# A hybrid decoder layer with mixture of experts on one core: sample states stored in eight pieces, step rows sent home one step later, the samples' chunk of the end added on VectorE

## The chip, the cores and the metric

The kernel runs on 1 core of a Trainium2 chip. The metric is the device time of one execution in microseconds, lower is better. TensorE does the matmuls (PE in the rows, PEld its weight loads), VectorE is DVE, ScalarE is ACT, GpSimd is POOL, SyncE is SP. SPq and POOLq are the queues of these engines where they issue DMAs.

## The reference, cut to what matters

One layer, 1024 prompt tokens and 8 sample tokens of 1024 features, all in float32. A mixer (mLSTM heads and HGRN2 heads) comes first and updates, for the 8 samples, two matrix states of 4 heads, C and S, which are outputs. Then comes the mixture of experts, whose sum with the scaled input is normalised:

```python
x = _layer_norm(DEEPNORM_ALPHA * x + mix, ln1_g, ln1_b)
x = _layer_norm(DEEPNORM_ALPHA * x + _hmoe(x, ...), ln2_g, ln2_b)
...
a = jnp.einsum('nd,edf->nef', xt, w1)
u = jnp.einsum('nd,edf->nef', xt, w3)
hdn = jax.nn.silu(a) * u * gate[..., None].astype(x.dtype)
return jnp.einsum('nef,efd->nd', hdn, w2).reshape(B, T, D)
...
S_new = jnp.exp(G_end[:, :, 0, :])[..., None] * S + jnp.einsum('bhsc,bhsv->bhcv', k * jnp.exp(G_end - G), i)
```

Each token takes 2 of 16 experts (the other gates are zero), and an expert has three weights (gate, up, down) of 1 MB each.

## The kernel before

The first two thirds of the time are the mixer, the first layer norm and the router; the change does not touch them. What follows has two parts.

**The steps.** Pairs of token and expert are sorted by expert into tiles of 32 rows. 80 tiles make 20 steps (0 to 19) of four lanes: a step takes 128 rows, 32 on each of four streams, and each stream has its own expert. TensorE's order in step n (`tensor_moe`, `step`) is: gate product of n (L1359), transposes of the hidden rows of n-1 (L1345), transposes of the gathered rows of n+1 (L1321), down product of n-1 (L1336), up product of n (L1370). Weights have one buffer for each stream, so a load may be issued only when the product of the step before has read its buffer.

SyncE's order in step n (`sync_moe`, `step`) is: read the experts and flags of n+1 from SBUF into registers (`experts_of`, L1232), wait for gate product n, issue the four gate loads of n+1 (L1220), in even steps below 16 also the samples' v rows (`load_v`, L1241); read the experts of n, wait for down product n-1, issue the four down loads of n (L1226); wait for up product n, issue the four up loads of n+1 (L1223). Each of these loads has a flag: it moves its 1 MB only if the stream changes its expert there, so many issues move nothing. All of SyncE's DMAs are on one queue.

GpSimd (`pool_moe`) issues indirect DMAs: it gathers the rows of step n (L1460), then sends home the finished rows of step n-4 (`send_home`, L1453: 128 rows of 4 KB into the DRAM tensor `y_rows`). A send waits for VectorE's sum of its step (L1584) and for the send before it. There are four buffers for finished rows. ScalarE fills the one of step n (`scale_x`, L1407) once step n-4 has arrived home, and the gather of n+2 waits for that fill. ScalarE's next instruction is the SiLU of step n (L1417).

VectorE updates four heads' worth of the sample states at the end of each of the steps 0 to 15 (`update_state`, L1593 to L1595): C in steps 0 to 7, S in steps 8 to 15. Each is 2 MB, 16 KB on each partition. C is stored whole ahead of step 8 and S ahead of step 16 (`between`, L1277 to L1284, issued in the helper at L470), each after a wait for the last of its updates. Ahead of step 12 the parameters of the last layer norm are loaded (L1281).

**The end.** When all 20 sends have arrived, SyncE loads nine chunks of pairs of rows (L1295): the 8 sample rows first, then eight chunks of 128 tokens, 1 MB each. TensorE adds the two rows of a pair by products with the identity (L1383), 4 products of 512 columns a chunk, each with two records in the trace, and VectorE takes the statistics (L1633, L1635) and centres (L1636); ScalarE and GpSimd finish chunks 0 to 6 in that order, VectorE the last two (L1639), and SyncE stores them.

Of the kernel before, what the change touches and what calls it, by code (L numbers as in the profile page):

```python
# [20 lines left out]
ALU = mybir.AluOpType  # L21
# [10 lines left out]
H = 4  # L32
DV1 = P + 1
PIECE = NT // 3
HB = H * NS
LEVELS = [64, 32, 16, 8, 4, 2, 1]
NLEV = len(LEVELS)
NTT = NCH + 1
# [10 lines left out]
STEPS = (2 * NT + NE * (ROWS - 1)) // ROWS // STREAMS  # L49
# [61 lines left out]
def _program(nc, t, ctx):  # L111
# [15 lines left out]
    PS = ctx.enter_context(nc.psum_tensor("psum", [P, 8, 512], F32))  # L127
# [5 lines left out]
    ident, ones = const("ident"), const("ones")  # L133
# [335 lines left out]
    def out_dma(eng, dst, src):  # L469
        eng.dma_start(dst, src).then_inc(s.outputs, 16)  # L470
        outs[0] += 1
# [41 lines left out]
    def x_rows(c):  # L513
        return P if c < NCH else NS
# [699 lines left out]
    def sync_moe(sp):  # L1214
        wg = t["w_gate"].rearrange("e (p k) f -> e p k f", k=KD)
        wu = t["w_up"].rearrange("e (p k) f -> e p k f", k=KD)
        wd = t["w_down"].rearrange("e (p k) n -> e p k n", k=2)

        def load_gate(q, expert, new):
            sp.dma_start(w_gate[q], wg[bass.ds(expert, 1)].rearrange("e p k f -> p (e k) f"), cond=new).then_inc(s.w_gate_in, 16)  # L1220

        def load_up(q, expert, new):
            sp.dma_start(w_up[q], wu[bass.ds(expert, 1)].rearrange("e p k f -> p (e k) f"), cond=new).then_inc(s.w_up_in, 16)  # L1223

        def load_down(q, expert, new):
            sp.dma_start(w_down[q], wd[bass.ds(expert, 1)].rearrange("e p k n -> p (e k) n"), cond=new).then_inc(s.w_down_in, 16)  # L1226

        def experts_of(n):

            def words(w, top):  # L1230
                row = step_loads[0:1, bass.ds((n * 2 + w) * STREAMS, STREAMS)]
                return nc.values_load_multi_w_load_instructions(row, engines=[mybir.EngineType.SP], min_val=0, max_val=top,  # L1232
                                                                skip_runtime_bounds_check_because="experts are minima with NE - 1, flags come from a comparison")[1]

            experts, flags = words(0, NE - 1), words(1, 1)
            return [(q, experts[q], flags[q]) for q in range(STREAMS)]

        def load_v(piece):
            if piece >= 1:
                sp.wait_ge(s.state_added, 2 * piece)  # L1240
            sp.dma_start(v_piece, v_dram[piece:piece + 1].rearrange("a (b v) -> a b v", b=NS).partition_broadcast(P).rearrange("p a b v -> p (a b) v")).then_inc(s.v_piece_in, 16)  # L1241

        sp.wait_ge(s.experts_known, 1)
        sp.wait_ge(s.mixed, NTT)
        first = experts_of(0)
        for q, expert, _ in first:
            load_gate(q, expert, None)
        sp.wait_ge(s.slots_part, AFTER_SPREAD[0] + 1)
        for q, expert, _ in first:
            load_up(q, expert, None)  # L1250
        for q, expert, _ in first:
            load_down(q, expert, None)
        early_outs.append(outs[0])

        def step(pair, i, last):
            n = pair * 2 + i
            if not (last and i == 1):
                coming = experts_of(n + 1)
                sp.wait_ge(s.gate_done, pair * 2 + (i + 1))
                for q, expert, new in coming:  # L1260
                    load_gate(q, expert, new)
                if i == 0 and pair < 2 * H:
                    load_v(pair)
            if not is_first(pair, i):
                present = experts_of(n)
                sp.wait_ge(s.down_done, n)
                for q, expert, new in present:
                    load_down(q, expert, new)
            if not (last and i == 1):
                sp.wait_ge(s.up_done, pair * 2 + (i + 1))  # L1270
                for q, expert, new in coming:
                    load_up(q, expert, new)

        def between(pair):

            if pair == 4:
                sp.wait_ge(s.outputs, 16 * early_outs[0])  # L1277
                sp.wait_ge(s.state_added, 8)
                out_dma(sp, t["out_C_s"].rearrange("p h b v -> p (h b) v"), C0)
            elif pair == 6:  # L1280
                sp.dma_start(ln2_gb, t["ln2"].partition_broadcast(P)).then_inc(s.ln2_in, 16)  # L1281
            elif pair == 8:
                sp.wait_ge(s.state_added, 16)
                out_dma(sp, t["out_S_s"].rearrange("p h b v -> p (h b) v"), S0)  # L1284

        for pair in range(STEPS // 2):
            between(pair)
            for i in range(2):
                step(pair, i, pair == STEPS // 2 - 1)
        sp.wait_ge(s.outputs, 16 * outs[0])  # L1290
        sp.wait_ge(s.y_out, 16 * STEPS)
        homes = y_rows[0:SPARE].rearrange("(k n) d -> n k d", k=2)
        for n, c in enumerate(ROW_ORDER):
            r = x_rows(c)
            sp.dma_start(pair_of[c][0:r], homes[c * P:c * P + r]).then_inc(pair_in[n], 16)  # L1295
        for n, c in enumerate(ROW_ORDER):
            r = x_rows(c)
            if n < Y_SHIFTED:
                sp.wait_ge(s.y_ready, n + 1)
            else:  # L1300
                sp.wait_ge(s.y_last, NCH + n - Y_SHIFTED)
            out_dma(sp, t["out_y"][c * P:c * P + r], pair_of[c][0:r, 0])
        sp.wait_ge(s.outputs, 16 * outs[0])

    def tensor_moe(pe):
# [67 lines left out]
        pairs_loop(pe, step)  # L1373
        turn_hid(STEPS - 1)
        down(STEPS // 2 - 1, 1)
        for n, c in enumerate(ROW_ORDER):
            r = x_rows(c)
            pe.wait_ge(pair_in[n], pair_there[n])
            if n >= 4:
                pe.wait_ge(s.y_centred, n - 3)  # L1380
            for half in range(2):
                for k in range(2):
                    m = mm(PS[0:r, 2 * (n % 4) + half, :], ident[0:r, 0:r], pair_of[c][0:r, k, half * 512:(half + 1) * 512], start=(k == 0), stop=(k == 1))  # L1383
            m.then_inc(s.y_summed, 1)

    def scalar_moe(act, link, tell):
# [52 lines left out]
    def pool_moe(pool, link, tell):  # L1439
        g = nc.gpsimd  # L1440
        pool.wait_ge(s.tiles_known, 1)
        pool.wait_ge(s.x1_written, 16 * NTT)

        pool.wait_ge(s.routed, NTT)
        pool.wait_ge(s.outputs, 16 * early_outs[0])

        def send_home(n):

            pool.wait_ge(s.y_read, 2 * n + 2)
            if n >= 1:  # L1450
                pool.wait_ge(s.y_out, 16 * n)
            off = bass.IndirectOffsetOnAxis(slot_home[:, n:n + 1].bitcast(U32), 0)
            g.indirect_dma_start(y_rows, off, ysb[n % YBUFS], None).then_inc(s.y_out, 16)  # L1453

        for n in range(STEPS):
            if n >= 2:
                pool.wait_ge(s.xg_turned, n - 1)
                pool.wait_ge(s.x_scaled, n - 1)
            off = bass.IndirectOffsetOnAxis(slot_tok[:, n:n + 1].bitcast(U32), 0)
            g.indirect_dma_start(xg[n % 2], None, x1_dram, off).then_inc((s.xg_in0, s.xg_in1)[n % 2], 16)  # L1460
            if n >= 4:
                send_home(n - 4)
        for n in range(STEPS - 4, STEPS):
            send_home(n)

        pool.wait_ge(s.ln2_in, AFTER_FIRST + 16)
        for n, c in enumerate(ROW_ORDER[:Y_SHIFTED]):
            y = pair_of[c][0:x_rows(c), 0]
            pool.wait_ge(s.lstd_ready, NTT + n + 1)
            tell(g.tensor_tensor(y, y, ln2_gb[0:x_rows(c), 1], ALU.add), s.y_ready)  # L1470

    def vector_moe(dve, link, tell):
# [154 lines left out]
        for n, c in enumerate(ROW_ORDER):  # L1627
            r = x_rows(c)
            y = pair_of[c][0:r, 0]
            summed = PS[0:r, 2 * (n % 4):2 * (n % 4) + 2, :].rearrange("p a b -> p (a b)")  # L1630
            dve.wait_ge(s.y_summed, NTT + n + 1)
            for half in range(2):
                i = v.bn_stats(fst[0:r, c, half], summed[:, half * 512:(half + 1) * 512])  # L1633
            link(i)
            tell(v.bn_aggr(fmv[0:r, c], fst[0:r, c]), s.moments)  # L1635
            tell(v.scalar_tensor_tensor(y, summed, fmv[0:r, c, 0:1], ln2_gb[0:r, 0], ALU.subtract, ALU.mult), s.y_centred)  # L1636
            if n >= Y_SHIFTED:
                dve.wait_ge(s.lstd_ready, NTT + n + 1)
                tell(v.scalar_tensor_tensor(y, y, fsd[0:r, c:c + 1], ln2_gb[0:r, 1], ALU.mult, ALU.add), s.y_last)  # L1639
# [474 lines left out]
```

## Time and profile before

| | us |
| --- | --- |
| median of 3 runs | 1168.73 (1166.11 to 1173.96) |
| the profiled execution, its own time | 1177.88 |
| its span | 1176.0 |
| granted TensorE clock, mean share | 0.935 |
| TensorE busy (share of the span) | 1051.2 (89%) |
| VectorE busy | 541.5 (46%) |
| ScalarE busy | 274.3 (23%) |
| GpSimd busy | 214.2 (18%) |

The span is from the first to the last instruction of the profiled execution; positions in the rows are microseconds from its start. The steps take from about 818 to 1124, the end the rest. In the chain of waits every row is a start, a length and what the end of the execution hung on at that time.

### The profile page before, as it was taken

The numbers are of one execution on the slowest core, as the hardware profiler recorded it, in microseconds if no ns is written. First come the engines' busy times: TensorE is split into PE (matmuls) and PEld (weight loads), VectorE is DVE, ScalarE is ACT, GpSimd is POOL, SyncE is SP. The second block draws the span as 40 slices with busy tenths as digits, with TensorE's granted clock in tenths as the row PEclk, the third lists the DMA queues.
The fourth block names the chain that finished last, engine by engine and source line by source line (L and its number), as shares of the span: only waits on it lengthen the run. The fifth ranks groups of instructions, "written<-read, shape, count | busy, mean of one in ns | idle before, by whom it ended". The sixth has DMA issues, their size and how long they took to land.

```text
span 1176.0 us, 17325 instructions
## 1 busy us (share of the span) xinstructions
PE 1051.2 (89%) x6814; PEld 618.9 (53%) x6814; DVE 541.5 (46%) x983; ACT 274.3 (23%) x557; POOL 214.2 (18%) x204
## 2 busy tenths in 40 slices
PE   7999999979999987999999999942788889898877
PEld 4666666646565545566666656542344445444423
DVE  1540033344645466776685667353133324332227
ACT  1542112122222223233333333110111111111103
POOL 0000000001111132443453354000111101110014
PEclk9999999989999988999999999965898889898968
DMA  9110102020000154001100010508898776846765
GB/s 383 44 72 1 72 1 72 0 76 1 1 1 1 34 214 181 3 18 37 37 18 19 37 36 19 191 33 347 333 353 299 262 285 196 339 161 223 260 250 201
DMA packets 29443, 150.11 MB, mean 128 GB/s; under 512 B 5338, under 2 KB 5786, under 8 KB 20034
## 3 DMA queue, kind: packets, MB, share of 16 engines
q1 hardware_dynamic: 23186, 123.94, 28.1%
q0 software_dynamic: 5760, 20.97, 4.9%
q10 hardware_dynamic: 432, 4.35, 1.0%
q8 instruction: 38, 0.62, 0.2%
q14 instruction: 27, 0.22, 0.1%
HBM read 317.32 MB, written 23.82 MB: 290 GB/s over the span
## 4 chain that ended last, share of the span: by engine, by line
PE 83%; DMA 7%; DVE 5%; issue 3%; SPq 2%; ACT 0%; POOL 0%; DVEq 0%; ACTq 0%; POOLq 0%
PE psum L1689 18%; PE psum L1740 9%; PE psum L772 9%; PE psum L785 8%; PE psum L1336 5%; PE psum L1359 5%; PE psum L1370 4%; PE psum L813 4%; PE psum L1383 3%; DMA weight_slots<-in_w_gate 2%; DMA hg_decay<-in_w_up 2%; PE psum L747 1%; PE psum L1707 1%; DMA hg_q<-in_w_down 1%; PE psum L1321 1%
## 5 line engine op out<-in xcount | busy, mean ns | idle before, releaser
L1689 PE MATMUL psum<-x_cm,weight_slots 128*128 128x344 f32 x720 | 209.0, 453 | 0.0
L1689 PEld LDWEIGHTS psum<-x_cm,weight_slots 128*128 128x128 f32 x720 | 136.6, 190 | 71.9 <-issue 1.1
L1740 PE MATMUL psum<-weight_slots,x_cm 128*128 128x512 f32 x256 | 114.0, 599 | 0.0
L1359 PE MATMUL psum<-weight_slots,scratch 128*32 128x256 f32 x1280 | 83.6, 419 | 24.2 <-DMA weight_slots<-in_w_gate 14.9
L1336 PE MATMUL psum<-conv_qk,scratch 128*32 128x512 f32 x320 | 82.5, 663 | 16.6 <-issue 12.6
L1336 PE MATMUL psum<-hg_k,scratch 128*32 128x512 f32 x160 | 82.4, 663 | 0.0
L1336 PE MATMUL psum<-hg_q,scratch 128*32 128x512 f32 x160 | 82.4, 663 | 0.0
L1359 PEld LDWEIGHTS psum<-weight_slots,scratch 128*32 128x32 f32 x1280 | 45.6, 121 | 59.5 <-issue 20.9
L1740 PEld LDWEIGHTS psum<-weight_slots,x_cm 128*128 128x128 f32 x256 | 48.1, 193 | 54.5 <-issue 54.5
L1370 PE MATMUL psum<-conv_qk,scratch 128*32 128x256 f32 x640 | 72.6, 379 | 2.2 <-DMA hg_decay<-in_w_up 2.1
L1370 PE MATMUL psum<-hg_decay,scratch 128*32 128x256 f32 x640 | 72.6, 379 | 0.0
L813 PEld LDWEIGHTS psum<-scratch 128*128 128x128 f32 x448 | 58.7, 194 | 24.4 <-issue 22.7
L1025 POOL TENSOR_TENSOR scratch<-scratch,hg_k 128x256 f32<-128x256 f32 x56 | 45.5, 813 | 104.5 <-ACT scratch L924 104.3
L1460 POOL DMA_INDIRECT scratch<-x_rows,hg_k x20 | 19.4, 969 | 247.6 <-ACT x_cm L1407 89.4
L813 PE MATMUL psum<-scratch 128*128 128x128 f32 x448 | 59.8, 277 | 2.0 <-POOL scratch L1025 2.0
L1417 ACT ACTIVATE scratch<-psum 128x256 f32<-128x256 f32 x20 | 7.7, 384 | 224.9 <-PE psum L1359 224.9
L1966 DVE TENSOR_SCALAR scratch<-scratch,small 128x1024 f32<-128x1024 f32 x8 | 6.5, 814 | 114.8 <-ACT scratch L1825 114.8
L1113 DVE COPY_PREDICATED scratch<-level_masks,psum 128x512 f32<-128x512 uint8 x64 | 47.1, 736 | 25.6 <-PE psum L815 22.4
L772 PE MATMUL psum<-weight_slots,x_cm 128*128 128x512 f32 x128 | 58.2, 598 | 0.0
L1370 PEld LDWEIGHTS psum<-conv_qk,scratch 128*32 128x32 f32 x640 | 37.9, 110 | 38.6 <-issue 8.8
L772 PE MATMUL psum<-conv_qk,x_cm 128*128 128x512 f32 x128 | 57.8, 594 | 0.0
L924 ACT ACTIVATE scratch<-scratch 128x512 f32<-128x512 f32 x56 | 35.4, 632 | 94.0 <-DVE scratch L1108 93.8
(376 smaller groups left out, 1645.8 us busy)
## 6 DMA issues: line engine op xcount, KB each, us to landing
weight_slots<-in_w_gate SPq DMA_DIRECT2D x80, 1024.0 KB
conv_qk<-in_w_up SPq DMA_DIRECT2D x40, 1024.0 KB
hg_decay<-in_w_up SPq DMA_DIRECT2D x40, 1024.0 KB
conv_qk<-in_w_down SPq DMA_DIRECT2D x40, 1024.0 KB
hg_k<-in_w_down SPq DMA_DIRECT2D x20, 1024.0 KB
hg_q<-in_w_down SPq DMA_DIRECT2D x20, 1024.0 KB
weight_slots<-in_w_in SPq DMA_DIRECT2D x6, 2048.0 KB, 8.3
x_cm<-in_xT SPq DMA_DIRECT2D x8, 516.0 KB, 7.9
```

The source lines that it names most:

```text
L772: i = mm(PS[:, bank, :], xT[:, k, c * P:(c + 1) * P], w_slot(g)[:, k, :], start=(k == 0), stop=(k == KD - 1))
L785: i = mm(PS[:, 6 + n, :], lhs, w_out[:, e, n * 512:(n + 1) * 512], start=(e == 0), stop=(e == 7))
L813: i = mm(hp(2 + n % 2, h), xl[:, h], xl[:, h], start=True, stop=True)
L924: tell(A(xlev[n % 2], xlev[n % 2], ACT.Exp), s.level_exp)
L1025: tell(g.tensor_tensor(x, x, y, ALU.mult), s.level_scaled)
L1113: tell(v.copy_predicated(amat, msk[:, l:l + 1, :].to_broadcast([P, H, P]), by_h(PS[:, 2 + n % 2, :])), s.level_kept)
L1336: m = mm(PS[lane, 5 + half, :], hidT[:, k, lane], w_down[q][:, k, half * 512:(half + 1) * 512], start=(k == 0), stop=(k == 1))
L1359: m = mm(PS[lane, 2, 0:FF], xgT[i][:, k, lane], w_gate[q][:, k], start=(k == 0), stop=(k == KD - 1))
L1370: m = mm(PS[lane, 3, 0:FF], xgT[i][:, k, lane], w_up[q][:, k], start=(k == 0), stop=(k == KD - 1))
L1383: m = mm(PS[0:r, 2 * (n % 4) + half, :], ident[0:r, 0:r], pair_of[c][0:r, k, half * 512:(half + 1) * 512], start=(k == 0), stop=(k == 1))
L1689: i = mm(PS[0:m, idx % 4, 0:PIECE], lhs_of(k), xT[:, k, n * PIECE:(n + 1) * PIECE], start=(k == 0), stop=(k == KD - 1))
L1740: i = mm(PS[:, bank, :], xT[:, k, c * P:(c + 1) * P], w_slot(g)[:, k, :], start=(k == 0), stop=(k == KD - 1))
```

## The change

The store of C ahead of step 8 and of S ahead of step 16 are taken out. In their place eight stores of 0.5 MB (4 KB on each partition) are issued in the odd steps 3, 5, ..., 17, each behind the four down loads and ahead of the wait for the up product: four pieces of C, then four of S. A piece waits for the update that was made two steps earlier. GpSimd sends home the rows of step n-5 behind the gather of step n, where it was n-4. At the end VectorE adds the pair of the samples' chunk (8 rows) itself, and TensorE begins with the first chunk of 128 tokens.

```diff
@@ sync_moe
+        def store_states(piece):
+            kind, at = piece // H, 8 * piece % HB
+            sp.wait_ge(s.state_added, 2 * piece + 2)
+            out_dma(sp, (t["out_C_s"], t["out_S_s"])[kind].rearrange("p h b v -> p (h b) v")[:, at:at + 8], (C0, S0)[kind][:, at:at + 8])
+
...
                 for q, expert, new in present:
                     load_down(q, expert, new)
+                if i == 1 and 1 <= pair <= 2 * H:
+                    store_states(pair - 1)
...
-            if pair == 4:
-                sp.wait_ge(s.outputs, 16 * early_outs[0])
-                sp.wait_ge(s.state_added, 8)
-                out_dma(sp, t["out_C_s"].rearrange("p h b v -> p (h b) v"), C0)
-            elif pair == 6:
+            if pair == 6:
                 sp.dma_start(ln2_gb, t["ln2"].partition_broadcast(P)).then_inc(s.ln2_in, 16)
-            elif pair == 8:
-                sp.wait_ge(s.state_added, 16)
-                out_dma(sp, t["out_S_s"].rearrange("p h b v -> p (h b) v"), S0)
@@ tensor_moe
-        for n, c in enumerate(ROW_ORDER):
-            r = x_rows(c)
+        for n, c in list(enumerate(ROW_ORDER))[1:]:
             pe.wait_ge(pair_in[n], pair_there[n])
-            if n >= 4:
+            if n >= 5:
                 pe.wait_ge(s.y_centred, n - 3)
...
-                    m = mm(PS[0:r, 2 * (n % 4) + half, :], ident[0:r, 0:r], pair_of[c][0:r, k, half * 512:(half + 1) * 512], start=(k == 0), stop=(k == 1))
+                    m = mm(PS[:, 2 * (n % 4) + half, :], ident, pair_of[c][:, k, half * 512:(half + 1) * 512], start=(k == 0), stop=(k == 1))
@@ pool_moe
-            if n >= 4:
-                send_home(n - 4)
-        for n in range(STEPS - 4, STEPS):
+            if n >= 5:
+                send_home(n - 5)
+        for n in range(STEPS - 5, STEPS):
             send_home(n)
@@ vector_moe
-            summed = PS[0:r, 2 * (n % 4):2 * (n % 4) + 2, :].rearrange("p a b -> p (a b)")
-            dve.wait_ge(s.y_summed, NTT + n + 1)
+            if n == 0:
+                summed = y
+                dve.wait_ge(pair_in[n], pair_there[n])
+                link(v.tensor_tensor(y, y, pair_of[c][0:r, 1], ALU.add))
+            else:
+                summed = PS[:, 2 * (n % 4):2 * (n % 4) + 2, :].rearrange("p a b -> p (a b)")
+                dve.wait_ge(s.y_summed, NTT + n)
```

SyncE's queue between the up loads of step 8 (issued in step 7) and the gate loads of step 9, before. `out_C_s` is the output of state C, `hg_k` holds the experts and flags, `hg_decay` and `conv_qk` the up weights, `weight_slots` the gate weights:

```order
L1226 DMA hg_q<-in_w_down 128x2048
L1223 DMA conv_qk<-in_w_up 128x2048 x2
L1223 DMA hg_decay<-in_w_up 128x2048 x2
L470 DMA out_C_s<-x_cm 128x4096
L1232 TENSOR_LOAD hg_k x2
L1220 ISA
L1220 DMA weight_slots<-in_w_gate 128x2048
```

The same place with the change:

```order
L1226 DMA hg_q<-in_w_down 128x2048
L470 DMA out_C_s<-x_cm 128x1024
L1223 DMA conv_qk<-in_w_up 128x2048 x2
L1223 DMA hg_decay<-in_w_up 128x2048 x2
L1232 TENSOR_LOAD hg_k x2
L1220 ISA
L1220 DMA weight_slots<-in_w_gate 128x2048
```

The store has a quarter of the elements and stands ahead of the up loads; between the up loads and the reads of the experts nothing is left.

GpSimd's queue at the start of the steps, before (`x_rows` is gathered, `y_rows` is home):

```order
L1460 DMA scratch<-x_rows,hg_k 128x1024 x5
L1453 DMA y_rows<-scratch,hg_k 4224x1024
L1460 DMA scratch<-x_rows,hg_k 128x1024
L1453 DMA y_rows<-scratch,hg_k 4224x1024
L1460 DMA scratch<-x_rows,hg_k 128x1024
```

And with the change:

```order
L1459 DMA scratch<-x_rows,hg_k 128x1024 x6
L1452 DMA y_rows<-scratch,hg_k 4224x1024
L1459 DMA scratch<-x_rows,hg_k 128x1024
L1452 DMA y_rows<-scratch,hg_k 4224x1024
L1459 DMA scratch<-x_rows,hg_k 128x1024
```

The first send stands behind six gathers instead of five.

TensorE's last rows before, the additions of the end:

```order
L1383 MATMUL psum<-scratch,constants 8x512 x4
L1383 MATMUL psum<-x_cm,constants 128x512 x16
L1383 MATMUL psum<-weight_slots,constants 128x512 x16
```

And with the change:

```order
L1382 MATMUL psum<-x_cm,constants 128x512 x16
L1382 MATMUL psum<-weight_slots,constants 128x512 x16
```

The four products on 8 rows are gone; VectorE has one addition of 8x1024 elements more.

## Rows read from the trace of the kernel before

**Rows 1.** The page's chain by engine; a stretch: engines' busy time, clock, DMA share, GB/s

```profile
PE 83%; DMA 7%; DVE 5%; issue 3%; SPq 2%; ACT 0%; POOL 0%; DVEq 0%; ACTq 0%; POOLq 0%
860.00:880.00 20.00, 17.02 (x242) 9.05 (x238) 6.15 (x10) 2.48 (x4) 3.41 (x4) 1.00 0.96 353
```

**Rows 2.** Chain of waits around the store of C: start, length, what

```profile
938.42 3.49 PE psum L1370 x64
...
944.61 0.35 SPq L470
945.00 1.78 SPq L1232
946.82 3.32 SPq L1232
951.47 7.72 DMA weight_slots<-in_w_gate
959.23 6.52 PE psum L1359 x64
```

**Rows 3.** Chain of waits in the two steps ahead of the store of S, and around it

```profile
1041.62 3.45 PE psum L1370 x64
1045.07 3.45 PE psum L1359 x64
...
1053.43 3.50 PE psum L1370 x64
...
1059.59 0.35 SPq L470
1059.98 1.78 SPq L1232
1061.79 3.27 SPq L1232
...
1066.67 7.61 DMA weight_slots<-in_w_gate
1074.32 5.31 PE psum L1359 x64
```

**Rows 4.** The reads of the experts: duration ns min/median/max; the stretch of the store of S

```profile
L1232 SPq TENSOR_LOAD <-hg_k x77: 862/869/3320, 795.4 to 1102.4; - x77
1060.00:1064.00 4.00, 4.00 (x42) 2.01 (x38) 1.12 (x2) 2.02 (x3) 0.00 (x0) 1.00 0.93 393
```

**Rows 5.** Chain of waits: loads that came late at steps 13 and 18

```profile
1003.98 10.07 DMA weight_slots<-in_w_gate
...
1088.82 8.08 DMA hg_decay<-in_w_up
```

**Rows 6.** A fill, the gather and the send behind it, in order of time; landing of the sends

```profile
967.61 1.14 ACT L1407 ACTIVATE x_cm<-scratch,hg_k 128x1024 f32<-128x1024 f32 x1
969.50 0.96 POOL L1460 DMA_INDIRECT scratch<-x_rows,hg_k  x1 [16.66 <-ACT x_cm L1407]
972.28 0.98 POOL L1453 DMA_INDIRECT y_rows<-scratch,hg_k  x1 [1.82 <-DVE scratch L1584]
DMA to landing us min/median/max: 3.3/8.1/10.8
```

**Rows 7.** The end: loads and their landing, TensorE's additions, clock (column before the last two)

```profile
1116.96 6.20 PE psum L1336 x32
1122.00:1124.00 2.00, 1.12 (x12) 0.16 (x4) 0.82 (x2) 0.00 (x0) 0.00 (x0) 0.98 0.00 0
1128.53 2.40 SPq L1295 DMA_DIRECT2D x_cm<-y_rows  x4
DMA to landing us min/median/max: 5.7/12.7/18.9
1130.69 6.99 PE L1383 MATMUL psum<-scratch,constants 8*8 8x512 f32 x8 [7.57 <-DMA scratch<-y_rows]
1142.00:1144.00 2.00, 2.00 (x5) 0.91 (x4) 0.14 (x1) 0.00 (x0) 2.00 (x1) 0.86 1.04 416
```

## Prediction

> **What bounds the kernel now.** I read four views in this order. First the page's chain of waits: TensorE holds 83% of it, and the part that a rearrangement can reach is the 7% of DMA, 2% of SyncE's queue and 3% of issue; nearly all of that lies in the steps and the end [rows 1]. Second the chain in order of time, which shows what each gap of TensorE hangs on [rows 2, 3, 5]. Third the reads of the experts and the sends in their own views [rows 4, 6]. Last the end by stretches, with the granted clock [rows 7].
>
> A step in which nothing is late takes 11.81 us: up product to up product, 1041.62 to 1053.43 [rows 3]. So in the steps TensorE is the bound as long as the weights are there in time, and the DMA engines are the second bound close behind (96% of them busy from 860 to 880, [rows 1]).
>
> **What the two stores cost now.** The chain runs from SyncE's store of C (944.61), which waited for VectorE's last update, over the two reads of the experts of step 9 (945.00 and 946.82) to the gate loads (issued until 951.47, landed 7.72 later), and to the gate product of step 9 at 959.23 [rows 2]. Three things are added up there. SyncE stood at the wait until 944.6, 2.7 us after the up product at 938.42 had ended. Its two reads took 1.78 + 3.32 = 5.1 us, where such a pair takes 2 x 0.869 = 1.74 [rows 4]. And the gate loads lay behind 2 MB of store on the same queue, which at the 393 GB/s of the stretch of the other store is 2.1 / 0.393 = 5.3 us [rows 4]. The same three stand at the store of S [rows 3].
>
> In time of TensorE: without anything late gate product 9 would begin one step and one product after up product 7: 938.42 + 11.81 + 3.45 = 953.68. It began at 959.23, 5.55 us later [rows 2, 3]. It then took 6.52 instead of the 3.45 of the one at 1045.07, because the clock had fallen in the gap: 3.07 more. Together 8.6 us for C. For S: due at 1053.43 + 15.26 = 1068.69, begun at 1074.32, 5.63 late, and 5.31 - 3.45 = 1.86 of slow product: 7.5 us.
>
> **What the change takes away and gives.** Stores: the gate loads of steps 9 and 17 are issued as soon as the gate product of the step before has read the buffers. That is 3.45 + 3.45 us after the start of the up product ahead of it: 945.3 and 1060.3, instead of about 951.5 and 1066.7. The slowest single load of 1 MB elsewhere in a like place took 8.08 us from issue to landing [rows 5]; with 1.3 us for issuing four loads (from the end of the reads at 950.14 to 951.47) the last would land by 954.7 and 1069.7 at worst, 1.0 us after the product is due, and at best in time. That so short a gap lets the clock fall no row here says (the two that did were 5.6 us long); I take 0.5 for C and 0 for S. Gain: 8.6 - 0.5 = 8.1 and 7.5.
>
> The eight pieces: each adds an issue of 0.35 us [rows 2] and a wait on an update that is two steps old, so no wait. Behind the piece on SyncE's queue are only the up loads of the next step, and SyncE waits for the up product there anyway; that wait hides the issue. If the cover were gone it would be 8 x 0.35 = 2.8 us. Not hidden are the bytes: 0.52 MB / 393 GB/s = 1.3 us of DMA time ahead of the up loads. Bounds for each piece are 0 (DMA idle there) and 1.3 us (that load is late already). Where the trace has a load late just behind a piece it counts: the up load of step 18 (issued until 1088.82, 8.08 to landing, in the chain), behind the last piece: 1.3 us. The gate loads of step 13 (1003.98, 10.07 to landing) come two queue entries behind the piece of step 11, with the layer norm's 1 MB between: 0 to 1.3, I take 0.7. In the crowded stretch up to step 4 the first piece brings 0.5 MB, and the later send takes 0.5 MB out: 0, with 1.3 either way. The other four stand where no chain row names a load: 0.
>
> Reads of experts behind a piece: they now come after the up loads. If they were slowed in proportion to the bytes (3.36 us more for 2 MB, so 0.84 for 0.5 MB), they would still end inside the gate product's 3.45 us [rows 3]. I take 0; the price without that cover is a rival below.
>
> Sends: a send now follows 1.1 us behind the next gather instead of 2.8 us (972.28 against 969.50) and belongs to one step earlier [rows 6]. Its 0.5 MB move from the time of the down loads to that of the gate loads. A late down load may gain, a gate load lose, at most 1.3 us each; I take 0 for the sum and, as if two or three of either kind were left over, 3 us either way for the range. At the last four sends nothing moves, since they stand in the loop behind the gathers in both.
>
> The end: the loads of the chunks are issued from 1128.53, and the first chunk of 128 rows lands 5.7 us later, at 1134.2 [rows 7]. TensorE is then still in the products on 8 rows, until 1130.69 + 6.99 = 1137.7, and only then begins the chunks, which run without a gap to the end. Without those products it begins at 1134.2. That is 3.4 us earlier, if the slow part of the chunks stays as long. The clock share over 1142 to 1144 is 0.86, so it rose at about 1142.6, 5.0 us after the first full chunk began, and 11.9 after the first product on 8 rows. After the gap before 1116.96, full products had it at 1122.1: 5.1 us. So the row says that 5 us of full products raise it and that the 8-row products did nothing for it; the slow part stays, and 3.4 us is the gain. VectorE's addition of 8x1024 is done long before TensorE's first chunk. The low bound: if the clock rose 11.9 us after the first product whatever it is, it would rise at 1146.2, some 7 more products would be slow, and the gain would be 0.
>
> The Trainium skill (TensorE: Matmul & The Clock Gate, section "What's actually happening") says that the clock is set by how busy TensorE has been recently. By that rule the 8-row products, which keep it busy for 7 us, would already have raised the clock, and to take them away would cost the warming. This trace does not agree: the share was still at half speed when they ended and until 1142.6.
>
> Sum: 8.1 + 7.5 + 3.4 - 1.3 - 0.7 = 17.0 us. The profiled execution's own time is 1177.88, so it would be 1160.9. The median of the runs shown is 9.15 us below that execution; taking the same 17.0 off the median gives 1151.7. That the unprofiled runs are shorter may mean that loads land sooner in them and the two gaps are smaller. If the gate load landed 4 us after its issue instead of 7.7, each gap would be 3.6 shorter, and the gain of the stores 15.6 - 7.2 = 8.4, the whole 9.8 and the time 1158.9. That is the long side of the range. On the short side are C without the 0.5, no price for pieces, and 3 us from the sends: 8.6 + 7.5 + 3.4 + 3 = 22.5, so 1146.2; with the spread of the medians (1166.1 to 1174.0) I go to 1144.
>
> **The rivals.**
> 1. The DMA engines take it back. The bytes are the same, and if the steps are bound by them, a gap that goes at step 9 comes back at the next change of experts. For it: 96% busy from 860 to 880 [rows 1]. Against: after both stores the chain is TensorE's alone for a step and more, and a step needs no load where no stream changes. Price: 1.3 us at four of the eight pieces, once with a fall of the clock (3.1), 8.3 instead of the 2.0 that I took: gain 17.0 - 6.3 = 10.7, time 1158.0. With it go the smaller gaps of the unprofiled runs above: the same region.
> The Trainium skill (DMA: Bandwidth & Descriptors, section "Issuing engines are not separate DMA queues") says that DMAs of all issuing engines share the same 16 engines. By it the sends of GpSimd do not get out of SyncE's way by being on another queue, which is this rival's case; no row here separates the two.
> 2. Each piece slows the reads behind it, and the cover is not there: 8 x 0.84 = 6.7 us. Gain 10.3, time 1158.4. For it: the 1.78 and 3.32 [rows 2]; against it: the pieces are ahead of the up loads.
> 3. Slower than before: the sends become the loop that sets the pace. A fill takes 1.14 us, the gather follows 0.75 later and takes 0.96, the send would follow 0.1 later and take 0.98, then it lands after L, and only then comes the next fill: 3.9 + L [rows 6]. A step takes (1074.32 - 959.23) / 8 = 14.4 us on average, 13.5 without the gap at S [rows 2, 3]. The loop is longer than that from L = 9.6 on; the median landing is 8.1, the longest 10.8 [rows 6]. A fill has room: the one at 967.61 came 1.9 us after its gate product (959.23 + 6.52), and ScalarE is wanted again at the end of the next, so it could end 8.8 us later. Over the 14 steps that have a gather and a send this moves the point to a mean landing of 10.2. If every landing took 13 us because gather, send and gate loads now come together, it is 14 x (16.9 - 13.5) - 8.8 = 39 us lost: 1191. At 11.4 the whole gain is gone.
> 4. The end gives nothing (clock rises late, as above): 17.0 - 3.4 = 13.6, time 1155.1.
>
> **How the numbers follow.** Forecast 0.60 (1151.7), rival 1 with the small gaps 0.22 (1158), rival 2 0.05 (1158.4), rival 3 0.05 (1191), rival 4 0.08 (1155.1). A measurement of this kernel tells about 1% from no change, 11.7 us, so the border is 1157.0. Forecast and rival 4 are mostly on the faster side (0.65 of their 0.68), of rivals 1 and 2 about a third (0.09); the rest of these four is within 1% (0.21), and rival 3 is slower, or within 1% in its mild form: 0.04 and 0.01. That gives 0.74, 0.22 and 0.04. The range from 1144 to 1163 takes in the forecast with its bounds, rivals 1, 2 and 4, and leaves out rival 3 and a little at both ends.
>
> **What would show it.** Right: no gap of TensorE before gate products 9 and 17, and both at 3.45 us; no read of the experts over about 2 us; the first L1382 product at about 5.7 us after the loads' issue, with the clock rising some 5 us later; the chain at the up load of step 18 longer by about 1 us. Wrong: gaps of the same sum at other steps (rival 1), reads of 1.7 us or more behind every piece with gate loads late (rival 2), ScalarE's fills waiting for sends that land after more than 10 us (rival 3), the clock rising 12 us after the end's first product (rival 4).

## The result, and the profile after

| | before | changed |
| --- | --- | --- |
| median, us | 1169.33 (1166.11 to 1173.96, 4 runs) | 1152.89 (1152.44 to 1154.9, 4 runs) |
| ratio, 95% interval | | 0.986, 0.9824 to 0.9895 |
| span of the profiled execution | 1176.0 | 1150.9 |
| granted clock, mean share | 0.935 | 0.947 |

The change takes 16.4 us off the median (interval 12.3 to 20.6); 17.0 were forecast. The spans of the two profiled executions differ by 25.1 us, because the one of before was 8.5 us above its median and the one of after stands at its own. So a trace pair shows where gaps went, and only the timed runs say how much a gap is worth.

The chain by engine of the changed kernel, which answers to the first row of [rows 1]:

```profile
PE 86%; DMA 5%; DVE 4%; issue 3%; SPq 1%; ACT 0%; POOL 0%; DVEq 0%; ACTq 0%; POOLq 0%
```

The chain of waits of the changed kernel around gate product 9 (at 952.42) and gate product 17 (at 1056.32), against [rows 2] and [rows 3]:

```profile
937.16 3.45 PE psum L1370 x64
940.61 3.45 PE psum L1359 x64
...
948.96 3.45 PE psum L1370 x64
952.42 3.45 PE psum L1359 x64
...
1052.87 3.45 PE psum L1370 x64
1056.32 3.45 PE psum L1359 x64
```

Up product to gate product without a gap, both times, and both at 3.45 us: the two gaps of 5.6 us and their slow products are gone. The reads of the experts, against [rows 4]: the longest is now 2.06 us instead of 3.32.

```profile
L1232 SPq TENSOR_LOAD <-hg_k x77: 862/868/2055, 794.3 to 1085.9; - x77
```

What is late now, from the chain: the gate load of step 13, the up load of step 18, and the products behind them. They answer to [rows 5]:

```profile
995.31 10.13 DMA weight_slots<-in_w_gate
1005.48 4.91 PE psum L1359 x64
...
1068.98 9.72 DMA hg_decay<-in_w_up
1078.75 5.35 PE psum L1370 x64
```

The up load of step 18 takes 9.72 us instead of 8.08, and its product now runs partly at the slow clock. The table has the gaps of TensorE in the steps from down product 1 on (those ahead of it, at gate products 1 and 2, are the same in both within 0.1 us). An entry is the idle time ahead of the product plus, where it ran partly at the slow clock, what it took over its undisturbed 3.45 us (gate, up) or 3.57 (down). They are read off the chain and TensorE's timeline, in us:

| product that was late | before | changed |
| --- | --- | --- |
| down 1, up 2, down 2 | 3.4 | 6.3 |
| down 4 | 6.2 | 4.6 |
| down 6 | 6.7 | 5.8 |
| gate 9 | 8.6 | 0 |
| down 9 | 0.8 | 1.3 |
| gate 13, down 13 | 11.0 | 7.3 |
| gate 17 | 7.5 | 0 |
| up 18 | 0.6 | 4.2 |
| down 19 | 6.3 | 1.2 |
| sum | 51.1 | 30.7 |

That is 20.4 us; with 3.6 from the end and 0.9 from ahead of the steps it makes up 24.9 of the 25.1 of the spans. No trace below of a kernel with the pieces has a gap at gate 9 or 17, and every one with VectorE's addition has the shorter end; most of the other entries differ from run to run of one kernel.

The end of the changed kernel, against [rows 7]: first, by the timeline, the issue of the loads, VectorE's addition and TensorE's first products:

```profile
1107.03 2.44 SPq L1295 DMA_DIRECT2D x_cm<-y_rows  x4
1109.33 1.21 DVE L1632 TENSOR_TENSOR scratch<-scratch 8x1024 f32<-8x1024 f32 x1 [6.35 <-DMA scratch<-y_rows]
1112.73 2.07 PE L1382 MATMUL psum<-x_cm,constants 128*128 128x512 f32 x2 [11.09 <-DMA x_cm<-y_rows]
```

Then the busy time by stretch around it (the granted clock is the column before the last two):

```profile
1112.00:1114.00 2.00, 1.27 (x2) 0.76 (x3) 1.36 (x2) 1.01 (x3) 0.00 (x0) 0.50 1.02 416
...
1116.00:1118.00 2.00, 2.00 (x4) 0.79 (x3) 0.00 (x0) 0.00 (x0) 1.12 (x1) 0.68 1.03 414
```

TensorE begins 5.7 us after the loads' issue, as soon as the first chunk has landed. The share of 0.68 over 1116 to 1118 puts the rise of the clock at 1117.3, 4.6 us after the first full product. From the landing of the last send to the end of the span it is 44.3 us, where it was 47.9.

The landing of the sends, against [rows 6]:

```profile
DMA to landing us min/median/max: 3.3/6.5/11.1
```

### The profile page after: what moved, and what is told of

The parts are those of the page before. It is cut to its first block, busy times and chain, and to the rows that moved or that the text cites. A ratio compares the mean times of both kernels' runs of the same rounds, so it can differ in the third digit from the quotient of the medians.

```text
span 1150.9 us, 17314 instructions
## 1 busy us (share of the span) xinstructions
PE 1034.7 (90%) x6806; PEld 616.9 (54%) x6806; DVE 542.5 (47%) x984; ACT 274.7 (24%) x557; POOL 214.2 (19%) x204
## 4 chain that ended last, share of the span: by engine, by line
PE 86%; DMA 5%; DVE 4%; issue 3%; SPq 1%; ACT 0%; POOL 0%; DVEq 0%; ACTq 0%; POOLq 0%
PE psum L1693 18%; PE psum L772 10%; PE psum L1744 10%; PE psum L785 8%; PE psum L1336 6%; PE psum L1359 6%; PE psum L1370 5%; PE psum L813 4%; PE psum L1382 2%; PE psum L747 2%; PE psum L1711 1%; DMA hg_q<-in_w_down 1%; PE psum L1321 1%; DMA weight_slots<-in_w_gate 1%; DMA hg_decay<-in_w_up 1%
## 5 line engine op out<-in xcount | busy, mean ns | idle before, releaser
L1336 PE MATMUL psum<-conv_qk,scratch 128*32 128x512 f32 x320 | 79.3, 641 | 15.0 <-issue 10.0
L1359 PE MATMUL psum<-weight_slots,scratch 128*32 128x256 f32 x1280 | 77.4, 395 | 13.4 <-issue 8.7
L1336 PE MATMUL psum<-hg_k,scratch 128*32 128x512 f32 x160 | 79.1, 641 | 0.0
L1336 PE MATMUL psum<-hg_q,scratch 128*32 128x512 f32 x160 | 79.1, 641 | 0.0
L1744 PEld LDWEIGHTS psum<-weight_slots,x_cm 128*128 128x128 f32 x256 | 47.9, 192 | 54.3 <-issue 54.3
L1912 POOL TENSOR_TENSOR scratch<-scratch,constants 128x512 f32<-128x512 f32 x8 | 10.2, 1275 | 256.8 <-ACT scratch L1885 256.8
```

What stands on the lines that cost most here:

```text
L1336: m = mm(PS[lane, 5 + half, :], hidT[:, k, lane], w_down[q][:, k, half * 512:(half + 1) * 512], start=(k == 0), stop=(k == 1))
L1359: m = mm(PS[lane, 2, 0:FF], xgT[i][:, k, lane], w_gate[q][:, k], start=(k == 0), stop=(k == KD - 1))
L1744: i = mm(PS[:, bank, :], xT[:, k, c * P:(c + 1) * P], w_slot(g)[:, k, :], start=(k == 0), stop=(k == KD - 1))
```

## The experiments

All ratios are against the kernel before, run on the same chip beside them: its median was 1169.32 beside e1 to e4, 1173.19 beside e5 to e8 and 1171.13 beside e9 to e12. The changed kernel itself stood beside e9 to e12 alone. "Gap" is TensorE's idle time ahead of a product.

**e1: the pieces alone.** Sends and end as before.

```diff
+                if i == 1 and 1 <= pair <= 2 * H:
+                    store_states(pair - 1)
...
-                out_dma(sp, t["out_C_s"].rearrange("p h b v -> p (h b) v"), C0)
...
-                out_dma(sp, t["out_S_s"].rearrange("p h b v -> p (h b) v"), S0)
```

> The kernel before with the eight state pieces alone; sends and the end as before. Theory (the two whole stores held the gate loads of steps 9 and 17 back; two gaps of 5.6 us and their slow products, 15.6 us, go, 2.0 come back at steps 13 and 18): 13.6 us less than before, ratio 0.988; no gap ahead of gate products 9 and 17. Rival 1 (DMA takes it back): the same two gaps gone, but gaps of 6 to 8 us more at later loads, 7 us less than before, ratio 0.994.

Measured: 1156.48 against 1169.32, ratio 0.989 (0.9852 to 0.9928), 12.8 us less, with an interval of 8.4 to 17.3. Its chain, gate product 9 at 945.54, gate product 17 at 1050.19, and the up load of step 18:

```profile
942.09 3.45 PE psum L1370 x64
945.54 3.45 PE psum L1359 x64
...
1046.74 3.45 PE psum L1370 x64
1050.19 3.45 PE psum L1359 x64
...
1062.84 9.98 DMA hg_decay<-in_w_up
```

No gap at either gate, and the up load late by 2.5 us instead of 0.6. The expected 13.6 stands, and rival 1 (7 us) lies outside the interval. The trace is that of the fastest of the six runs, 8.3 us below their median, so most runs were later somewhere than it shows. Its longest read of the experts took 3.15 us, behind the piece of step 9:

```profile
L1232 SPq TENSOR_LOAD <-hg_k x77: 862/867/3151, 792.8 to 1078.4; - x77
```

**e2: the sends alone.**

```diff
-            if n >= 4:
-                send_home(n - 4)
+            if n >= 5:
+                send_home(n - 5)
```

> The kernel before with the sends home one step later alone. Theory (the sends change only which loads they meet): within 3 us of before either way, ratio 0.997 to 1.003. Rival 3 (sends as the loop that sets the pace): slower by 5 us or more, ScalarE's fills late behind landings over 10 us. A rival seen after the result (the smaller last gap, ahead of down product 19, comes from the sends): 3 to 5 us less than before, with that gap near 1 us.

Measured: 1165.95 against 1169.32, ratio 0.9971 (0.9943 to 0.9998), 3.4 us less. The last gap was 3.9 us in its trace, not near 1, so the sends alone do not make it small. The gain is at the edge of what was expected and just outside no change; rival 3 is out.

**e3: the end alone.**

```diff
+                link(v.tensor_tensor(y, y, pair_of[c][0:r, 1], ALU.add))
...
-        for n, c in enumerate(ROW_ORDER):
+        for n, c in list(enumerate(ROW_ORDER))[1:]:
```

> The kernel before with VectorE's addition of the samples' chunk alone. Theory (the 8-row products only kept TensorE from the first full chunk, and did not raise the clock): 3.4 us less than before, ratio 0.997; from the landing of the last send to the end of the span 44.3 us instead of 47.9. Rival 4 (clock rises about 12 us after the first product of the end, whatever it is): no change.

Measured: 1168.3 against 1169.32, ratio 0.9987 (0.9958 to 1.0016). By the clock of the timed runs this is unclear: 3.4 us is inside the interval and so is nothing. The traces are sharper, since the end hangs on nothing that is late by chance: 43.9 us from the last landing to the end of the span instead of 47.9. The five traces with the 8-row products (before, e1, e2, e4, e5) have 47.4 to 47.9 there, and the seven with VectorE's addition have 43.9 to 44.7 (changed, e3, e6, e8 to e11; e7 and e12 add products on 128 rows there).

**e4: whole stores behind the down loads** of steps 9 and 17.

```diff
+                if i == 1 and pair in (4, 8):
+                    sp.wait_ge(s.state_added, 2 * pair)
+                    name, state = (("out_C_s", C0), ("out_S_s", S0))[pair // 8]
+                    out_dma(sp, t[name].rearrange("p h b v -> p (h b) v"), state)
```

> The kernel before with both stores whole (2 MB), but in steps 9 and 17 behind the down loads and ahead of the up loads. If the place in the queue was the cost (wait, slow reads and bytes ahead of the gate loads), the gaps at gate products 9 and 17 go; the up loads of steps 10 and 18 lie behind 2 MB: step 10 changes no expert and loses nothing, the up load of step 18 comes 5.3 us later than before, a gap of about 6 us with 2 us of slow product. Net 15.6 - 7.5 = 8 us less than before. If the number of pieces matters as such, it is not faster than e1 by more than noise anyway; if bytes alone matter (rival 1), nothing is gained against before.

Measured: 1159.92, ratio 0.9932 (0.9904 to 0.996), 8 us less (9.4 by the medians). The chain behind the store of S:

```profile
1064.18 13.34 DMA hg_decay<-in_w_up
1077.56 6.18 PE psum L1367 x64
```

The gaps at the gates are gone, and the up load of step 18, which here lies behind 2 MB, takes 13.34 us: 5.3 more than the 8.08 of [rows 5], which is the transfer of the store. It makes a gap of 5.9 us and 2.7 us of slow product. So here the store of S costs its own transfer at the next load that moves bytes. The store of C shows no such price: behind it in e4 no product is more than 2.0 us late until gate product 13, and that one (down 9) waits for a load ahead of the store. How much of the gain over e4 comes from cutting the stores to pieces is not settled: e1 is 3.4 us below it by the medians, and the two intervals overlap.

**e5: a quarter of the bytes in the old place.**

```diff
-                out_dma(sp, t["out_C_s"].rearrange("p h b v -> p (h b) v"), C0)
+                out_dma(sp, t["out_C_s"].rearrange("p h b v -> p (h b) v")[:, 0:8], C0[:, 0:8])
```

(the same for S).

> The kernel before, both stores in their old place with their old waits, but of a quarter of the bytes (0.5 MB; three quarters of the states are not stored). It parts the three costs of the old place: the wait (2.7 us), the slow reads of the experts, the bytes ahead of the gate loads (5.3 us for 2 MB). If the reads are slow as long as the store runs, the pair takes about 2.6 us instead of 5.1, the gate loads are issued 2.5 us earlier and have 1.3 us of bytes ahead instead of 5.3: gaps at gate products 9 and 17 of 1 to 2 us instead of 5.6. If any store makes the pair 5.1 us, gaps of 3 us or more stay.

Measured: 1155.32, ratio 0.9848 (0.9791 to 0.9906). SyncE's and VectorE's part of its chain:

```profile
943.90 0.35 SPq L470
944.29 1.56 SPq L1232
945.88 0.87 SPq L1232
...
948.47 7.93 DMA scratch<-sample_v_rows
956.43 0.70 DVE weight_slots L1593
```

The pair of reads takes 2.43 us instead of 5.1, the gate loads are issued by 948.4, and gate product 9 is 0.2 us late and gate product 17 not at all, where 1 to 2 us were expected. So with a quarter of the bytes the wait for the update makes no gap at the gates; ahead of the whole store it is part of the chain of [rows 2], and no run has the whole store there without the wait. What does come is a gap of 2.5 us at down product 8, with 1.5 of slow product: the samples' v rows, the next entry of the queue (`load_v`), are late, and VectorE stands at its update and copies the hidden rows (L1603) only afterwards. These v rows lie behind the wait and the store, so the wait may cost something there.

**e6: 8-row products in the idle time of the end**, and **e7: full products there**, both on the changed kernel.

```diff
         down(STEPS // 2 - 1, 1)
+        for _ in range(6):
+            mm(PS[0:8, 0, :], ident[0:8, 0:8], cst[0:8, 0:512], start=True, stop=True)
```

```diff
         down(STEPS // 2 - 1, 1)
+        for _ in range(10):
+            mm(PS[:, 0, :], ident, cst[:, 0:512], start=True, stop=True)
```

> The changed kernel with six products of 8 rows and 512 columns (constants, into a bank nobody reads) behind the last down product, so that TensorE is busy for about 10 us of its 11 us of idle time. Theory (8-row products do not raise the clock): the clock stays at half speed until some 5 us into the full chunks, time as the changed kernel's (1152.9), from the last send's landing to the end 44.3 us. The skill's rule as I took it (any busy TensorE raises it): clock up before the first chunk, 2 to 2.5 us less.

> The changed kernel with ten full products (128x128 weights, 512 columns, constants, into a bank nobody reads) in the same place. Theory (5 us of full products raise the clock): it rises in the idle time, the chunks run at 3.44 us each from the first on, from the last send's landing to the end 42 us instead of 44.3; ratio 0.998 against the changed kernel. If the clock depended on the time since the gap alone, no difference to e6.

Measured: e6 1154.13 (1153.89 to 1156.9), ratio 0.9848 (0.9793 to 0.9904), 44.5 us from the last landing to the end; e7 1151.28 (1149.51 to 1153.06), ratio 0.982 (0.9779 to 0.9862), 42.1 us. Rows of e6's timeline: the extra products, and the first products of the first full chunk.

```profile
1103.02 8.12 PE L1377 MATMUL psum<-constants 8*8 8x512 f32 x12
1114.26 4.64 PE L1384 MATMUL psum<-x_cm,constants 128*128 128x512 f32 x5 [3.13 <-DMA x_cm<-y_rows]
```

The stretches of e6 in which the extra products begin, the one in which that chunk begins, and the one in which the clock rises:

```profile
1102.00:1104.00 2.00, 2.00 (x15) 0.42 (x8) 0.86 (x2) 0.00 (x0) 0.00 (x0) 1.00 0.00 0
1104.00:1106.00 2.00, 2.00 (x6) 0.39 (x4) 0.43 (x1) 0.00 (x0) 0.96 (x1) 0.84 0.00 0
1106.00:1108.00 2.00, 2.00 (x4) 0.26 (x2) 0.00 (x0) 0.00 (x0) 0.00 (x0) 0.50 0.65 262
...
1114.00:1116.00 2.00, 1.74 (x2) 0.84 (x3) 0.78 (x1) 1.16 (x2) 0.00 (x0) 0.50 1.03 422
...
1118.00:1120.00 2.00, 2.00 (x5) 0.89 (x4) 0.00 (x0) 0.00 (x0) 0.50 (x1) 0.74 1.01 410
```

The same rows of e7's timeline:

```profile
1100.58 8.85 PE L1377 MATMUL psum<-constants 128*128 128x512 f32 x20
1111.79 2.41 PE L1384 MATMUL psum<-x_cm,constants 128*128 128x512 f32 x5 [2.35 <-DMA x_cm<-y_rows]
```

And the stretches of e7 ahead of and at the start of the extra products, and just behind that chunk's start:

```profile
1098.00:1100.00 2.00, 2.00 (x12) 0.54 (x8) 0.00 (x0) 0.00 (x0) 0.00 (x0) 0.54 0.00 0
1100.00:1102.00 2.00, 2.00 (x12) 0.70 (x5) 1.29 (x2) 0.00 (x0) 0.00 (x0) 1.00 0.00 0
...
1112.00:1114.00 2.00, 2.00 (x5) 0.84 (x5) 0.45 (x1) 1.15 (x1) 0.15 (x1) 1.00 1.02 418
```

In e6 the clock was at full speed when the 8-row products began, straight behind down product 19. It fell some 2.3 us later (the share of 0.84 over 1104 to 1106), while TensorE was busy without a gap, and stayed at half speed until after the chunks had begun. In e7 down product 19 ran partly slow, and the clock had risen just ahead of the ten full products, so these did not raise it: they kept it at full speed until the chunks came. That is worth 2.2 us of the end in this trace, and e7's runs all lie below e6's. But e12, which has the same ten products, did not keep it (below).

**e8: the norm's parameters ahead of step 14**, on the changed kernel.

```diff
-            if pair == 6:
+            if pair == 7:
                 sp.dma_start(ln2_gb, t["ln2"].partition_broadcast(P)).then_inc(s.ln2_in, 16)
```

> The changed kernel with the load of the last norm's parameters (1 MB) ahead of step 14 instead of step 12, where it stands between the up loads of step 12 and the gate loads of step 13. If its bytes are what makes gate product 13 late (gap of 3.9 us and 1.3 us of slow product in the changed kernel), the gap shrinks by up to 2.6 us and the slow part goes: 3 to 4 us less than the changed kernel, about 1149.5. If the gap comes from the two gate loads themselves, no change.

Measured: 1149.22 (1145.8 to 1153.35), ratio 0.9806 (0.9761 to 0.9851). Beside it on the chip stood e6, which is the changed kernel but for products in idle time; e8 is 4.9 us below it, and all its runs are below e6's, which bears out the expected 3 to 4 us. Against the changed kernel's own ratios the intervals overlap. The gap at gate 13 shrank from 3.9 to 0.6 without a slow product. What is late next stands in its chain:

```profile
995.37 10.27 DMA scratch<-sample_v_rows
1009.12 3.67 PE psum L1336 x32
```

Again the v rows, queued behind the gate loads: VectorE waits for them, and down product 12 begins 1.8 us late, up product 13 another 1.3.

**e9 to e12, four kernels on one chip:** the changed kernel again, the same without the eight pieces, the same with the old sends, and e7 and e8 together. The edits of e10 and e11 on the changed kernel:

```diff
-                if i == 1 and 1 <= pair <= 2 * H:
-                    store_states(pair - 1)
```

```diff
-            if n >= 5:
-                send_home(n - 5)
+            if n >= 4:
+                send_home(n - 4)
```

> The changed kernel once more, as the reference of the three kernels beside it on this chip. Both theories: 1153, ratio to before 0.986.

> The changed kernel without the eight pieces (the samples' states C and S are not stored). It prices what the pieces still cost. Prediction's price: 2.0 us (1.3 at the up load of step 18, 0.7 at the gate load of step 13). If pieces cost nothing: 0. If each costs its 1.3 us of DMA time (rival 1): 8 to 10 us less than the changed kernel. The gap at the up load of step 18, 2.3 us in the changed kernel against 0.6 before, should go back to 0.6, and the last gap, ahead of down product 19, back from 1.2 to some 3.5 with a slow product, if the earlier gap is what gives the last load its time.

> The changed kernel with the sends in their old place (step n-4 behind the gather of n). From e2 alone (3 us less than before) the sends should be worth 0 to 3 us here too: 1153 to 1156. If they only pay while the whole stores are there, or the gap ahead of down product 2 that they bring (3.8 us and a slow product in the changed kernel, 1.9 without slow product in e1) weighs as much: 1150 to 1153.

> The changed kernel with the ten full products ahead of the end (e7) and the norm's parameters two steps later (e8). The two work at different places and should add: 1.6 to 2.3 us from e7, 3.7 from e8, together 5 to 6 us less than the changed kernel, about 1147.3, ratio to before 0.981.

| | median (range) | ratio to before (interval) |
| --- | --- | --- |
| e9 changed again | 1152.02 (1146.63 to 1160.11) | 0.9839 (0.9797 to 0.9881) |
| e10 no pieces | 1149.1 (1145.47 to 1150.08) | 0.9811 (0.9783 to 0.9838) |
| e11 old sends | 1151.86 (1148.21 to 1159.84) | 0.983 (0.98 to 0.9861) |
| e12 e7 and e8 together | 1148.83 (1141.24 to 1151.25) | 0.9804 (0.977 to 0.9838) |

The pieces still cost 2.9 us by the medians, with overlapping ranges. The chain of e10 at the up load of step 18 and at the last down product:

```profile
1064.91 7.96 DMA hg_decay<-in_w_up
1072.91 3.66 PE psum L1368 x64
...
1089.72 2.21 issue
1091.93 5.02 PE psum L1334 x32
```

Without the last piece the up load is late by 0.5 us, against 2.0 in e9 and 2.3 in the changed kernel. The last gap is 2.7 us with 1.5 slow, against 1.7 with 1.8 in e9 and 1.2 with none in the first trace of the changed kernel, so the second half of that expectation is not decided. The sends in their old place (e11) cost nothing that can be measured here, 0.2 us less by the medians; with ranges of 13.5 and 11.6 us the 3.4 us of e2 are not excluded. e12 is 3.2 us below e9 and not 5 to 6: its chain has the v rows as well.

```profile
991.80 8.81 DMA scratch<-sample_v_rows
...
1005.38 5.11 PE psum L1336 x32
```

The part of e7 did not come either. The clock was at full speed through the ten products, but fell just after the first chunk had begun, behind an idle time of 2.3 us as in e7:

```profile
1108.00:1110.00 2.00, 0.21 (x1) 0.21 (x2) 1.93 (x4) 0.50 (x2) 0.00 (x0) 1.00 1.01 410
1110.00:1112.00 2.00, 2.00 (x4) 0.95 (x4) 0.51 (x1) 1.15 (x1) 0.10 (x1) 0.68 1.03 422
1112.00:1114.00 2.00, 2.00 (x3) 0.67 (x2) 0.00 (x0) 0.00 (x0) 2.00 (x1) 0.50 1.03 416
```

From the last landing to the end it took 43.8 us, not 42.1. Against the kernel before e12 is faster beyond its interval, 19.0 to 26.9 us; its range overlaps e9's, and its median is as e8's.

## Why the prediction was right, and where not

**The two stores.** Predicted 15.6 us of gaps and slow products, with 2.0 taken back by the pieces. e1 gave 12.8 for 13.6, and no run with the pieces has a gap at gate 9 or 17. The mechanism stood: with no store right ahead of them the gate loads are in time. Of its three costs, e5 takes away three quarters of the bytes, which also shortens the reads, and the rest makes no gap at the gates; what the wait costs ahead of a whole store no run parts from the rest. e4 shows that the place decides which load pays for the bytes. The 0.5 us left for C rested on a slowest load of 8.08 us "elsewhere", though the trace of before has some of 8.48 and 10.65 us; the gate loads were in time all the same, and nothing was left. A clock that falls in short gaps was in that trace too: down products 13 and 4 ran partly slow behind 2.7 and 3.3 us.

**No fall back to DMA.** Rival 1 fell with e1, 12.8 us where it gave 7, and with e10: the pieces still cost 2.9 us by the medians where it gave 8 to 10.

**The price of the pieces.** The step "behind the last piece: 1.3 us" was mis-sized. The up load of step 18 took 9.5 to 10.0 us in the eight traces with the piece ahead of it and 8.0 to 8.2 in the five without a store there (before, e2, e3, e5, e10), so 1.3 to 2.0 more. TensorE's gap was 2.0 to 2.5 us instead of 0.5 to 0.7, and in three of the eight traces (changed, e9, e11) the product then ran partly slow, 1.9 us, which the prediction had at nothing. The 0.7 at gate product 13 is not parted: gap and slow product there were 6.6 us before, 5.3 in the changed kernel and 6.5 in e9, and 1.7 without pieces (e10), where down product 12 and up product 13 were late by 3.2 instead, behind the v rows. The whole price was 2.9 (e10 against e9, with overlapping ranges) for 2.0. Rival 2 costs nothing to be seen, but its premise was nearer than forecast: behind a piece of 0.5 MB single reads took up to 2.06 us in the changed kernel's trace, 3.15 in e1 and 3.19 in e9, where the prediction reckoned with 0.84 more for a pair. The pair ended 0.5 us past gate product 18 in the changed kernel and up to 1.6 past the gate product beside it in other traces, so the cover did not hold in full; but no gate product behind such a pair came late.

**The sends.** Taken at 0 with 3 either way. Alone they gave 3.4 us (0.2 to 6.7), on top of the other two parts nothing that can be measured (e11 against e9). What they moved shows at the start of the steps, where the prediction had 0: the gap ahead of up product 2 is 1.4 to 2.2 us in the six traces with the old sends and 0 to 0.8 in the eight with the later ones, and the gap ahead of down product 2 grew from 1.4 to 2.7 us to 2.7 to 4.6, with a partly slow product in five of the eight and in one of the six. The loop of rival 3 does not set the pace: the median landing went from 8.1 to 6.5 us, the longest from 10.8 to 11.1, and ScalarE's fills waited for a send 5 times, 4.2 us in all. Nothing in the chain hung on that. What the sends gained in e2 stays open.

**The end.** 3.4 us predicted, 3.6 measured in the changed kernel's trace and 4.0 in e3's. Rival 4 fell: the clock rose 4.6 us after the first full product, and in before and e6 it rose 4.9 and 4.8 us after the first full product, with 7 and 8 us of 8-row products ahead that did not raise it. The Trainium skill (TensorE: Matmul & The Clock Gate, section "What's actually happening") says that the clock is set by how busy TensorE has been; by that rule e6 should have been at full speed, and its trace does not agree: the clock fell from 1.00 to 0.50 while the 8-row products ran back to back.

**What was missed.** The last gap, ahead of down product 19, went from 6.3 us (3.7 of idle time, the rest slow product) to 1.2 in the trace, and no step of the prediction had it. Its idle time was 3.9 us in e2, 2.6 in e3, 2.7 in e10 and 3.5 in e12, and 1.1 to 1.7 in the other eight experiments. In all of these eight but e5 up product 18 comes 2.0 us late or more, which suggested that an early gap gives the last load its time; e12 has that early gap too, and 3.5 us at the end. The traces speak against a queue that empties: the load is the last of the down loads, issued at 1110.26 before and at 1093.77 with the change, and just ahead of these loads the DMA engines were nearly idle in both (before, then changed; the DMA share is the last column but one):

```profile
1106.90:1108.90 2.00, 2.00 (x30) 0.66 (x22) 0.19 (x1) 0.00 (x0) 0.00 (x0) 1.00 0.06 25
1090.40:1092.40 2.00, 2.00 (x29) 0.66 (x21) 0.19 (x1) 0.00 (x0) 0.00 (x0) 1.00 0.05 20
```

From that issue to the product it is 6.7 us before and 4.2 with the change, and 4.1 to 6.9 over all fourteen traces. Why the same load takes so different a time stays open.

The forecast of 17.0 against 16.4 therefore owes something to luck, to misses of both signs: the price of the pieces 0.9 too low by the medians, the sends and the last gap left out. For the profiled execution the same sum gave 1160.9, and it took 1152.7.

## What to carry to other kernels

A large store on the queue that also brings weights can cost its own transfer at the next load that moves bytes: 5.3 us for 2 MB in e4. Put it behind the load that is not due and ahead of one that mostly moves nothing; cut to pieces of 0.5 MB it left a load late by 2.0 to 2.5 us here instead of 5.9. Before taking away what is late, look up what is queued right behind it: here it was the samples' v rows, which came late next in e5, e8, e10 and e12.

## What the runs showed of the hardware that was not expected

Reads from SBUF into SyncE's registers take 0.87 us as a rule and are much longer while DMAs are busy, longest behind a store out of SBUF: 1.78 and 3.32 behind 2 MB, 1.56 and 0.87 behind 0.5 MB in e5, but 3.15 and 3.19 behind 0.5 MB in e1 and e9, and up to 3.46 in e4. Without a state store ahead of them they took up to 1.97 us (before, at 974.77) and 1.79 in e10, which has none.

Products on 8 rows with 512 columns kept TensorE busy for 7.0 us (before) and 8.1 us (e6) without raising its clock. In e6 it even fell, from 1.00 to 0.50, while they ran back to back with no idle time ahead of them. In both the granted clock rose only 4.8 to 4.9 us after the full products of the chunks had begun. Ten products on 128 rows in the same idle time kept it at full speed into the chunks in e7; in e12 it fell 0.9 us after the first chunk had begun. And a gap of 2.0 us ahead of up product 18 let the clock fall in e9, while one of 2.5 us in e1 did not.
